# Two heads in one attention step on halves of the matrix array, and adaLN products on four column strips

## The chip, the cores and the metric

The kernel runs on one core of a Trainium2 chip. The metric is device time in microseconds (us) of one execution. Of the kernel before, three runs are shown: 3553.65 us in the median, from 3548.11 to 3559.67. The engines are named as in the profile: PE is TensorE (PEld its weight loads), DVE is VectorE, ACT is ScalarE, POOL is GpSimd, and SP is SyncE, which here only issues transfers.

## What is computed

One inference step of a two-layer encoder trunk, for a prompt of 1024 frames and a sample of 32 frames, which share all weights (width D = 1024). All arithmetic is in fp32. Both groups stand side by side as T = 1056 columns. In short, from the reference:

```python
mod = silu(c) @ w_ada[i] + b_ada[i]                  # six vectors of 1024 per layer, 12 in all, for two rows c
sh1, sc1, gt1, sh2, sc2, gt2 = split(mod, 6)
h = rmsnorm(x, g[0]) * (1 + sc1) + sh1
y = mixer_ab(h) if i % 2 == 0 else mixer_c(h)        # A: 8 heads on 2 kv heads, sinks; B: mLSTM, 4 heads; C: 16 heads
x = x + gt1 * rmsnorm(y, g[1])
h = rmsnorm(x, g[2]) * (1 + sc2) + sh2
x = x + gt2 * rmsnorm(swiglu(h), g[3])

s = q @ k.T * d ** -0.5 + bias                       # attention, head_dim d = 64
m = max(s.max(-1), sink)                             # sink only in A
p = exp(s - m); p = p / (p.sum(-1) + exp(sink - m))  # softmax without sinks in C
o = p @ v
```

In A a block of 128 queries sees up to 256 keys, in C up to 640.

## The kernel before

**Layout and stages.** x, h and all activations lie transposed, features on the 128 partitions and frames along the columns. Projections split both operands into a high and a low part (fp32r) and run three matmuls per block of 128x352 (`project`, lines 670 to 683). The stages follow one another: the inputs are turned and the first norm and the first two adaLN vectors are made (lines 693 to 798); attention A in four pairs of heads (lines 900 to 908); the gates and the four heads of B; the output projection, residual and FFN of layer 0; attention C in eight pairs of heads (lines 1046 to 1082), each with the q, k and v projections of the next pair fed in between; the output projection and FFN of layer 1. Each engine runs a program of its own, written out by hand in the blocks `tensor`, `scalar`, `vector`, `gpsimd` and `sync`, and semaphores with computed counts tie them together.

**Attention.** A pair is two heads, whose q and k lie on partitions 0 to 63 and 64 to 127 of one tile. `attention` (lines 808, 1171 and 1632 on the three engines) takes 18 half steps: nine blocks of rows (eight of 128 prompt frames, one of 32 sample frames) for head 0, then the same for head 1. A half step is: scores on 64 rows of the array (line 824), DVE's reduction that adds the bias, writes the probabilities' exponents and takes the minimum (line 1666), in A another minimum with the sink (1670), ACT's exponential with its sum (1184) and in A a sink term (1183), PE's transposes of the probabilities, one for each block of 128 keys (838), ACT's copy of these to SBUF (1193 to 1196), the product with V, where the transposed probabilities are the stationary operand and 64 columns of V move (850), and DVE's reciprocal and scaling into `o_tok` (1649, 1651). Transposes lag the scores by two half steps in A and by one in C, the product with V by one more. At the end of a pair nine blocks of `o_tok` are turned in two rounds (863), and ACT and DVE write them as high part `o_hi` (1214) and low part `o_lo` (1679).

**What is fed in between.** `fill` is called once per half step on each engine. In A it runs half an adaLN product (`ada_fill`, `ada_products`, lines 763 and 877): the four or eight matmuls of silu(c) (two columns, the stationary operand) with 256 columns of w_ada (line 770). Four such products of eight matmuls make one of the 12 vectors. Their rows are copied by DVE (1522), turned in eight small transposes (781) and added to the bias (1527). Each product's weights are one tile of 1 MB that SP loads into a ring of four when the product four back is done (lines 408 to 414). In C, `fill` runs a third of a 352-column block of the next pair's projection (`qkv_step`, line 1035), and ACT evacuates each finished block (1428) and splits each new weight tile (1110), DVE its low part (1496). The first five fills stand in `pre` (1050 to 1067), between the transposes of the cached keys, of V and of K. The last C pair has no fill.

**Queues.** SP issues w_ada and all weight tiles in program order (lines 416 to 468). POOL loads the bias of each head: in A when the pair's scores are read (562), in C head 0's after nine half steps and head 1's after 18 (615).

Of the kernel before, what the change touches and what calls it, by code (L numbers as in the profile page):

```python
# [11 lines left out]
D = 1024  # L12
# [62 lines left out]
def build(nc, ins, outs):  # L75
# [3 lines left out]
    with ctx:  # L79
# [19 lines left out]
        XE = YF + 2 * HB_  # L99
# [18 lines left out]
        silu_c = small("silu_c", [128, KD, 2])  # L118
# [3 lines left out]
        mins = small("mins", [128, 6])  # L122
        sums = small("sums", [128, 6])
        rsum = small("rsum", [128, 6])
        neg_sink = small("neg_sink", [128, HQ_A])
        sink2 = small("sink2", [128, 2])
        sink_e = small("sink_e", [128, 6])
# [8 lines left out]
        ada_row = at("ada_row", [2, 4, 256], F0)  # L136
# [14 lines left out]
        probs_a = at("probs_a", [128, 3, 256], mx[0])  # L151
        probs = scratch("probs", [128, 2, 640])
        probs_t = scratch("probs_t", [128, 2, 5, 128])
        o_tok = scratch("o_tok", [128, NBLK + 1, 128])
# [47 lines left out]
        ADB = KD * 256 * 4  # L202
        ada_s = [at(f"ada_s{u}", [128, KD, 256], YF + ADB * u) for u in range(4)]
        ada_m = [at(f"ada_m{u}", [128, KD, 256], (YF, R1 + HB_ // 2)[u // 2] + ADB * (u % 2)) for u in range(4)]
# [60 lines left out]
        ada_loaded = [sem(f"ada_loaded{i}") for i in range(4)]  # L265
# [15 lines left out]
        t_done, t_read, o_done, o_read = sem("t_done"), sem("t_read"), sem("o_done"), sem("o_read")  # L281
# [29 lines left out]
        def one(n):  # L311

            return n + 1
# [28 lines left out]
        def key_blocks(kind, p):  # L343
# [8 lines left out]
            "A": dict(n0=0, r0=4, o0=0, pre=0, lag=2, score_bufs=3, fill0=0, probs=probs_a),  # L352
            "C": dict(n0=72, r0=4 + 72, o0=8, pre=4, lag=1, score_bufs=2, fill0=5, probs=probs),
# [9 lines left out]
        def score_bank(kind, n):  # L363
            return 1 + n % 3 if kind == "A" else 1 + 2 * (n % 2)
# [3 lines left out]
        def _(sp):  # L368
# [20 lines left out]
            ada = I["w_ada"].rearrange("l (k p) n -> l p k n", p=128)  # L389
# [18 lines left out]
            def ada_load(ring, layer, q, n):  # L408

                for u in range(4):
                    sp.wait_ge(ada_done, q * 4 + (n + u + 1))
                    c = bass.ds(q * 1024 + ((n + u) * 256 - layer * 6 * D), 256)
                    sp.dma_start(ring[u][:, :, :], ada[layer][:, :, c]).then_inc(ada_loaded[u], 16)

            ada_load(ada_s, 0, 0, 0)
            for i, c in enumerate((COL_KA, COL_VA)):
                load(i, i, plain(w_ab, i, slice(c, c + 128), KD))
            ada_load(ada_s, 0, 1, 0)
# [31 lines left out]
            ada_load(ada_m, 0, 0, 8)  # L451
            q_tile(2)
            ada_load(ada_m, 0, 0, 12)
            q_tile(3)
            with sp.Fori(1, 3) as q:
                ada_load(ada_m, 0, q, 12)
            ada_load(ada_m, 1, 3, 12)
            gates_tile()
            with sp.Fori(4, 6) as q:
                ada_load(ada_m, 1, q, 12)  # L460
            head_tile(0, 0)
            with sp.Fori(6, 9) as q:
                ada_load(ada_m, 1, q, 12)
# [62 lines left out]
        def _(pool):  # L526
# [12 lines left out]

            nc.gpsimd.memset(ones[:, :], 1.0).then_inc(const_done, 1)  # L540
# [26 lines left out]
            pool.wait_ge(ol_done, one(8))  # L567
# [71 lines left out]
            def pair_c(hp, par, last):  # L639
                if not last:  # L640

                    pool.wait_ge(ol_done, one(hp * 2 + 8))
                    apart(pool)
                    caches_c(hp + 1, 1 - par)
# [21 lines left out]
        def _(pe):  # L666
# [26 lines left out]
            pe.sem_inc(ada_done, 4)  # L693
# [67 lines left out]
            pe.wait_ge(const_done, 1)  # L761

            def ada_products(ring, m, half, bank_, copied, loads):

                u = m % 4
                if half == 0:
                    pe.wait_ge(ada_copied, copied)
                    pe.wait_ge(ada_loaded[u], loads)
# [3 lines left out]
                if half == 1:  # L772
                    last.then_inc(ada_done, 1)
# [1240 lines left out]
```

## Time and profile before

| | before |
|---|---|
| median of three runs | 3553.65 us (3548.11 to 3559.67) |
| profiled execution: span from the first to the last instruction | 3540.5 us |
| its own device time | not told apart from the three runs |
| PE busy | 3220.4 us (91%), 18909 matmul passes |
| DVE, ACT, POOL busy | 1218.8, 1037.2, 155.4 us |
| moved by DMA | 201.65 MB, mean 57 GB/s |
| mean granted clock of PE | 0.922 of full speed |

How to read it: a row of a timeline gives start, recorded length, engine, line of the kernel, operation, output<-inputs, shapes and a count. Recorded matmul lengths overlap their successors, so the start of the next group tells what a group cost in the queue. Two PE records stand for one fp32 matmul, three fp32r matmuls for one block of a projection. "128*2 128x256" means a stationary operand of 128 rows and two columns with 256 moving columns. What stands in square brackets is idle time before the instruction and what ended it. The granted clock is 1.00 at 2.4 GHz and 0.50 at 1.2 GHz.

### The profile page before, as it was taken

The numbers are of one execution on the slowest core, as the hardware profiler recorded it, in microseconds if no ns is written. First come the engines' busy times: TensorE is split into PE (matmuls) and PEld (weight loads), VectorE is DVE, ScalarE is ACT, GpSimd is POOL, SyncE is SP. The second block draws the span as 40 slices with busy tenths as digits, with TensorE's granted clock in tenths as the row PEclk, the third lists the DMA queues.
The fourth block names the chain that finished last, engine by engine and source line by source line (L and its number), as shares of the span: only waits on it lengthen the run. The fifth ranks groups of instructions, "written<-read, shape, count | busy, mean of one in ns | idle before, by whom it ended". The sixth has DMA issues, their size and how long they took to land.

```text
span 3540.5 us, 53095 instructions
## 1 busy us (share of the span) xinstructions
PE 3220.4 (91%) x18909; PEld 2904.5 (82%) x18909; DVE 1218.8 (34%) x2578; ACT 1037.2 (29%) x2090; POOL 155.4 (4%) x197
## 2 busy tenths in 40 slices
PE   6999988888679999999949999999994999999997
PEld 4655587787679999999948878788694999999996
DVE  3333333332442232323472222222227232323326
ACT  4322233333241111122243333333224212121123
POOL 2000000000100000000020000000002000000000
PEclk9999988877889999999969999999596999999998
DMA  9444212211101111111121111111020111111111
GB/s 307 134 138 135 89 34 26 26 19 69 36 24 38 51 42 51 45 39 57 36 75 47 41 38 38 38 38 38 13 85 12 42 47 43 52 33 56 48 33 64
DMA packets 279679, 201.65 MB, mean 57 GB/s; under 512 B 25932, under 2 KB 270356, under 8 KB 279156
## 3 DMA queue, kind: packets, MB, share of 16 engines
q1 hardware_dynamic: 271748, 166.31, 16.9%
q0 software_dynamic: 7792, 33.43, 2.8%
q8 instruction: 94, 1.54, 0.2%
q14 instruction: 45, 0.37, 0.0%
HBM read 181.49 MB, written 23.44 MB: 58 GB/s over the span
## 4 chain that ended last, share of the span: by engine, by line
PE 87%; DVE 6%; ACT 2%; issue 2%; DVEq 1%; DMA 1%; POOL 0%; SPq 0%; ACTq 0%; POOLq 0%
PE psum L679 22%; PE psum L680 21%; PE psum L681 21%; PE psum L824 6%; PE psum L770 5%; PE psum L850 5%; PE psum L838 3%; DVE x L1600 2%; DVE norm_buf L1557 1%; DVE diag L1548 1%; DVEq L1610 1%; ACT w_hi L1110 1%; PE psum L738 1%; PE psum L950 1%; PE psum L951 1%
## 5 line engine op out<-in xcount | busy, mean ns | idle before, releaser
L679 PE MATMUL psum<-h_hi,w_hi 128*128 128x352 f32 x3240 | 1081.4, 334 | 47.2 <-DVE w_lo L1496 19.1
L681 PE MATMUL psum<-h_hi,w_lo 128*128 128x352 f32 x3240 | 1053.0, 325 | 2.6 <-issue 2.6
L680 PE MATMUL psum<-h_lo,w_hi 128*128 128x352 f32 x3240 | 1053.4, 325 | 1.9 <-issue 1.9
L679 PEld LDWEIGHTS psum<-h_hi,w_hi 128*128 128x128 f32 x3240 | 620.0, 191 | 79.3 <-issue 31.0
L680 PEld LDWEIGHTS psum<-h_lo,w_hi 128*128 128x128 f32 x3240 | 621.6, 192 | 7.6 <-issue 7.6
L681 PEld LDWEIGHTS psum<-h_hi,w_lo 128*128 128x128 f32 x3240 | 619.3, 191 | 2.8 <-issue 2.8
L1496 DVE TENSOR_TENSOR w_lo<-w_raw,w_hi 128x1024 fp32r<-128x1024 f32 x231 | 282.2, 1224 | 698.1 <-ACT w_hi L1110 698.1
L679 PE MATMUL psum<-ff_hi,w_hi 128*128 128x352 f32 x1056 | 342.5, 324 | 3.9 <-DVE w_lo L1496 3.6
L1110 ACT ACTIVATE w_hi<-w_raw 128x1024 fp32r<-128x1024 f32 x231 | 242.5, 1053 | 353.6 <-PE psum L681 342.3
L680 PE MATMUL psum<-ff_lo,w_hi 128*128 128x352 f32 x1056 | 341.9, 324 | 0.0
L681 PE MATMUL psum<-ff_hi,w_lo 128*128 128x352 f32 x1056 | 341.9, 324 | 0.0
L679 PEld LDWEIGHTS psum<-ff_hi,w_hi 128*128 128x128 f32 x1056 | 199.6, 189 | 5.0 <-issue 5.0
L681 PEld LDWEIGHTS psum<-ff_hi,w_lo 128*128 128x128 f32 x1056 | 199.7, 189 | 0.0
L680 PEld LDWEIGHTS psum<-ff_lo,w_hi 128*128 128x128 f32 x1056 | 199.5, 189 | 0.0
L850 PE MATMUL psum<-v_tok,probs_t 128*128 128x64 f32 (+2 forms) x1264 | 179.7, 281 | 7.5 <-issue 5.7
L1184 ACT ACTIVATE probs<-probs,mins 128x128 f32<-128x128 f32 (+2 forms) x144 | 101.1, 702 | 285.2 <-DVE mins L1666 285.2
L1370 ACT ACTIVATE ff_hi<-ffs 128x352 f32 x126 | 62.8, 498 | 410.7 <-DVE ffs L1897 410.7
L850 PEld LDWEIGHTS psum<-v_tok,probs_t 128*128 128x128 f32 (+2 forms) x1264 | 166.1, 200 | 15.0 <-issue 11.3
L738 PE MATMUL psum<-diag,ones 128*128 128x128 f32 x144 | 37.4, 428 | 150.9 <-DVE diag L1548 150.9
L1897 DVE TENSOR_TENSOR ffs<-sil,psum 128x352 f32<-128x352 f32 x126 | 65.7, 521 | 310.5 <-PE psum L681 310.5
L1366 ACT ACTIVATE sil<-psum 128x352 f32<-128x352 f32 x126 | 58.6, 465 | 369.5 <-PE psum L681 369.5
L1666 DVE CUSTOM_DVE_ANT_0 probs<-psum,neg_bias 128x128 f32<-128x128 f32 (+2 forms) x144 | 95.6, 664 | 191.1 <-PE psum L824 175.0
(307 smaller groups left out, 3547.3 us busy)
## 6 DMA issues: line engine op xcount, KB each, us to landing
ada_m<-in_w_ada SPq DMA_DIRECT2D x40, 1024.0 KB, 5.2
w_raw<-in_w_ffn_gate SPq DMA_DIRECT2D x88, 192.0 KB
w_raw<-in_w_ffn_up SPq DMA_DIRECT2D x88, 192.0 KB
w_raw<-in_w_ffn_down SPq DMA_DIRECT2D x112, 128.0 KB
w_raw<-in_w_in_c SPq DMA_DIRECT2D x48, 192.0 KB
x<-x_spill POOLq DMA_DIRECT2D x2, 4224.0 KB, 12.8
ada_s<-in_w_ada SPq DMA_DIRECT2D x8, 1024.0 KB, 11.3
w_raw<-in_w_ffn_down SPq DMA_DIRECT2D x128, 64.0 KB
```

The source lines that it names most:

```text
L679: nc.tensor.matmul(out, w_hi[:, slot, k], hi[:, k, c], start=(k == 0), stop=False)
L680: nc.tensor.matmul(out, w_hi[:, slot, k], lo[:, k, c], start=False, stop=False)
L681: last = nc.tensor.matmul(out, w_lo[:, slot, k], hi[:, k, c], start=False, stop=(k == kt - 1))
L738: last = nc.tensor.matmul(psum[:, b0 + tt, c:c + 128], ones[:, :], diag[:, turn(n, tt) % 2, i], start=True, stop=True)
L770: last = nc.tensor.matmul(psum[0:2, bank_, 0:256], silu_c[:, k], ring[u][:, k, :], start=(k == 0), stop=(k == KD - 1))
L824: last = nc.tensor.matmul(psum[0:m, score_bank(kind, n) + col // 512, col % 512:col % 512 + kn], lhs, keys(blk, kn, rows, k, kct), start=T ...
L838: last = tr(tps[0:kn, s, 0:m], c["probs"][0:m, n % sb, 128 * s:128 * s + kn], ident[0:m, 0:m])
L850: last = nc.tensor.matmul(oacc[0:m, 0:64], probs_t[0:kn, n % 2, s, 0:m], v, start=(s == 0), stop=(s == len(kb) - 1))
L1110: A(w_hi[:, slot], w_raw[:, slot], ACT.Copy).then_inc(hi_done, 1)
L1184: A(probs[0:m, n % sb, 0:w], probs[0:m, n % sb, 0:w], ACT.Exp, scale=-1.0, bias=mins[0:m, n % 6:n % 6 + 1], accum_out=sums[0:m, n % 6:n % ...
L1496: V.tensor_tensor(w_lo[:, slot], w_raw[:, slot], w_hi[:, slot].bitcast(F32), ALU.subtract).then_inc(lo_done, 1)
L1666: op = V.tensor_tensor_reduce(out=probs[0:m, n % sb, 0:w], in0=sc, in1=neg_bias[0:m, e, c0:c0 + w], scale=1.0, scalar=3.0e38, op0=ALU.add, ...
```

## The change

**Attention.** A step now handles both heads of one block of rows, so a pair has nine steps and a tenth without scores. Scores of the two heads alternate, piece by piece, on rows 0 to 63 and 64 to 127, into PSUM banks 1-2 and 3-4. DVE reduces both, then waits for both exponentials and scales the probabilities themselves by the reciprocal of their sum (in A with the sink's term), before they are turned. The product with V has V (64 columns) as the stationary operand and the transposed probabilities as 128 moving columns; the two heads alternate on columns 0 to 63 and 64 to 127, and the output comes out already turned. `o_tok` and its final transposes are gone; ACT and DVE write `o_hi` and `o_lo` for one block of rows in every step. In A, the sink's term is the exponential of a difference (`sink_gap`) that DVE makes with one more small operation per step. Fills stand at two fixed spots per step (three in the first and last step of C). Transposes and product with V lag by one step in A and C alike.

**adaLN.** A slab of w_ada is now 128 rows by 1024 columns (0.5 MB, rows of 4 KB), in a ring of eight. A group is four matmuls of 256 columns, one per column strip of 32; silu(c) is padded with zeros to 32 columns. Eight groups make a vector, whose result lies on four strips and is turned in two transposes of 128x128. At the start all eight groups of the first vector run ahead of the first sum of squares, and all of the second after the third.

**Waits.** In C, POOL loads both heads' biases after the eighth step. Each pair's `pre` waits for the last copy of the pair before, not for its `o_lo`.

The core of the diff (the sizes of small buffers, semaphore counts of later stages and unchanged loops are cut):

```diff
-        ada_s = [at(f"ada_s{u}", [128, KD, 256], YF + ADB * u) for u in range(4)]
+        ada_s = [at(f"ada_s{k}", [128, D], YF + 4096 * k) for k in range(KD)]
...
+        FILLS = {"A": [(1, 2)] * 10, "C": [(0, 1, 2)] + [(1, 2)] * 8 + [(0, 1, 2)]}
...
+            def ada_load(ring, q):
+                for k in range(KD):
+                    if q:
+                        sp.wait_ge(ada_done, KD * (q - 1) + k + 1)
+                    sp.dma_start(ring[k][:, :], I["w_ada"][q // 6, 128 * k:128 * k + 128, D * (q % 6):D * (q % 6) + D]
+                                 ).then_inc(ada_loaded[k], 16)
...
-                    pool.wait_ge(scores_read, hp * 18 + (CREDIT + 72 - 18 + 9 * (e + 1)))
+                    pool.wait_ge(scores_read, hp * 18 + (CREDIT + 72 - 18 + 17 + e))
...
+            def ada_products(ring, q, k, bank_):
+                if k == 0:
+                    pe.wait_ge(ada_copied, one(q))
+                pe.wait_ge(ada_loaded[k], q * 16 + 16)
+                for u in range(4):
+                    last = nc.tensor.matmul(psum[32 * u:32 * u + 32, bank_, 0:256], silu_c[:, k], ring[k][:, 256 * u:256 * u + 256],
+                                            start=(k == 0), stop=(k == KD - 1))
+                last.then_inc(ada_done, 1)
...
+            for k in range(KD):
+                ada_products(ada_s, 0, k, 3)
+            sum_x(0, 0, 0)
+            ada_transposes(0, 5)
+            spread(0, 0, 0)
+            sum_x(0, 1, 0)
+            spread(0, 1, 0)
+            sum_x(0, 2, 0)
+            for k in range(KD):
+                ada_products(ada_s, 1, k, 4)
+            ada_transposes(1, 5)
+            spread(0, 2, 0)
...
@@ attention, tensor block @@
+                for i in range(10):
+                    if i < 9:
+                        m = qrows(i)
+                        pe.wait_ge(scores_read, N(i) * 2 + CREDIT)
+                        cuts = cut_scores(kind, i)
+                        col = 0
+                        for s, (blk, kn) in enumerate(cuts):
+                            for e in range(2):
+                                rows = slice(64 * e, 64 * e + 64)
+                                last = nc.tensor.matmul(psum[0:m, score_bank(e) + col // 512, col % 512:col % 512 + kn],
+                                                        q[rows, 128 * i:128 * i + m], keys(blk, kn, rows, k, kct), start=True, stop=True)
+                                if s == len(cuts) - 1:
+                                    last.then_inc(scores, 1)
+                            col += kn
+                    work(i, 0)
+                    if i:
+                        turned(i - 1, 0)
+                    work(i, 1)
+                    if i:
+                        turned(i - 1, 1)
+                    work(i, 2)
+                    if i:
+                        n, m = i - 1, qrows(i - 1)
+                        pe.wait_ge(t_read, R(2 * n + 2))
+                        pe.wait_ge(ol_done, one(N(n)))
+                        kb = key_blocks(kind, n)
+                        for s, (blk, kn) in enumerate(kb):
+                            for e in range(2):
+                                cols = slice(64 * e, 64 * e + 64)
+                                v = vc[0:kn, blk[1], cols] if isinstance(blk, tuple) else vt[0:kn, blk, cols]
+                                last = nc.tensor.matmul(oacc[cols, 0:m], v, probs_t[0:kn, e, s, 0:m],
+                                                        start=(s == 0), stop=(s == len(kb) - 1))
+                        last.then_inc(o_done, 1)
...
@@ attention, scalar block @@
+                for i in range(10):
+                    work(i, 0)
+                    if i:
+                        copy(i - 1, 0)
+                    if i < 9:
+                        exps(i, 0)
+                    work(i, 1)
+                    if i < 9:
+                        exps(i, 1)
+                    if i:
+                        copy(i - 1, 1)
+                    work(i, 2)
+                    if i:
+                        act.wait_ge(o_done, N(n) + 1)
+                        A(tile_of(o_hi, it)[:, :, 128 * n:128 * n + m], oacc[:, 0:m].unsqueeze(1), ACT.Copy).then_inc(oh_done, 1)
...
@@ attention, vector block, after the two reductions of step i @@
+                    if i < 9:
+                        dve.wait_ge(exp_done, N(i) * 2 + 2)
+                        V.reciprocal(rsum[0:m, b, :], total[0:m, b, :])
+                        for e in range(2):
+                            V.tensor_scalar(probs[0:m, b, e, 0:w], probs[0:m, b, e, 0:w], rsum[0:m, b, e:e + 1], None,
+                                            ALU.mult).then_inc(p_done, 1)
+                    work(i, 1)
+                    work(i, 2)
+                    if i:
+                        dve.wait_ge(oh_done, N(n) + 1)
+                        V.tensor_tensor(tile_of(o_lo, it)[:, :, cs], oacc[:, 0:m].unsqueeze(1), tile_of(o_hi, it)[:, :, cs].bitcast(F32),
+                                        ALU.subtract).then_inc(ol_done, 1)
```

## Rows read from the trace of the kernel before

**Rows 1.** The page: its span, and the chain that ended last by engine.
```profile
span 3540.5 us, 53095 instructions
...
PE 87%; DVE 6%; ACT 2%; issue 2%; DVEq 1%; DMA 1%; POOL 0%; SPq 0%; ACTq 0%; POOLq 0%
```

**Rows 2.** Windows: length; busy PE, PEld, DVE, ACT, POOL; granted clock; DMA share; GB/s.
```profile
27.00:104.00 77.00, 61.88 (x325) 41.86 (x323) 27.22 (x34) 37.03 (x50) 18.92 (x12) 0.89 0.88 280
206.00:273.00 67.00, 63.45 (x335) 31.38 (x333) 27.59 (x123) 19.79 (x77) 1.07 (x2) 0.98 0.52 163
629.00:639.00 10.00, 8.19 (x59) 6.45 (x58) 4.58 (x24) 5.47 (x24) 0.00 (x0) 1.00 0.00 1
1954.00:2039.00 85.00, 82.34 (x508) 67.86 (x507) 24.88 (x77) 33.67 (x76) 5.81 (x12) 1.00 0.14 40
2480.00:2572.00 92.00, 84.64 (x293) 59.39 (x293) 22.51 (x75) 25.80 (x64) 2.60 (x4) 0.51 0.04 12
```

**Rows 3.** The timeline of one half step of attention A, PE, ACT and DVE.
```profile
222.31 0.44 PE L838 MATMUL psum<-ident,probs_a 128*128 128x128 f32 x2
...
222.58 0.56 PE L850 MATMUL psum<-v_tok,probs_t 128*128 128x64 f32 x4
222.78 0.38 ACT L1193 ACTIVATE probs_t<-psum 128x256 f32<-128x256 f32 x1 [2.15 <-PE psum L838]
223.06 0.28 ACT L1183 ACTIVATE sink_e<-sink,mins 128x1 f32<-128x1 f32 x1
...
223.07 0.70 PE L824 MATMUL psum<-k_a,q_a 64*128 64x256 f32 x2
...
223.25 0.49 ACT L1184 ACTIVATE probs_a<-probs_a,mins 128x256 f32<-128x256 f32 x1
...
223.64 0.19 ACT L1184 ACTIVATION_READ_ACCUMULATOR probs_a<-probs_a,mins 128x1 f32 x1
...
223.69 1.89 PE L770 MATMUL psum<-ada_m,silu_c 128*2 128x256 f32 x8
223.95 0.42 DVE L1666 CUSTOM_DVE_ANT_0 probs_a<-psum,neg_bias 128x256 f32<-128x256 f32 x1
...
224.46 0.16 DVE L1670 TENSOR_TENSOR mins<-mins,sink 128x1 f32<-128x1 f32 x1
...
225.51 0.44 PE L838 MATMUL psum<-ident,probs_a 128*128 128x128 f32 x2
```

**Rows 4.** The PE timeline: the first scores and the last output transposes of one A pair.
```profile
205.73 0.46 PE L824 MATMUL psum<-k_a,q_a 64*128 64x128 f32 x2 [0.87 <-ACT q_a L1168]
...
271.31 1.14 PE L863 MATMUL psum<-ident,o_tok 128*128 128x128 f32 x4 [1.88 <-DVE o_lo L1679]
```

**Rows 5.** The PE timeline of a C step: scores of 512 columns, then projection matmuls.
```profile
2007.97 1.12 PE L824 MATMUL psum<-k_c,q_c 64*128 64x512 f32 x2
2009.02 0.43 PE L679 MATMUL psum<-h_hi,w_hi 128*128 128x352 f32 x1
2009.29 0.32 PE L680 MATMUL psum<-h_lo,w_hi 128*128 128x352 f32 x1
2009.44 0.32 PE L681 MATMUL psum<-h_hi,w_lo 128*128 128x352 f32 x1
```

**Rows 6.** Groups by line and shape: count, busy us, mean ns of one, idle before.
```profile
L1110 ACT ACTIVATE w_hi<-w_raw 128x1024 fp32r<-128x1024 f32 x231 | 242.5, 1053 | 353.6 <-PE psum L681 342.3 <-DMA w_raw<-in_w_in_ab 11.3
...
L1184 ACT ACTIVATE probs<-probs,mins 128x640 f32<-128x640 f32 x64 | 53.0, 829 | 144.6 <-DVE mins L1666 144.6
L1193 ACT ACTIVATE probs_t<-psum 128x640 f32<-128x640 f32 x64 | 44.5, 696 | 12.8 <-PE psum L838 12.8
...
L1774 DVE TENSOR_SCALAR conv_t<-u_k,conv_h 128x1059 f32<-128x1059 f32 x4 | 3.1, 773 | 24.4 <-issue 15.9 <-ACT q_b L1292 8.5
```

**Rows 7.** The PE timeline of the start: third sum of squares, products of the second vector.
```profile
47.38 0.83 PE L719 MATMUL psum<-ones,norm_buf 128*128 128x1 f32 x6
...
55.17 10.52 PE L770 MATMUL psum<-ada_s,silu_c 128*2 128x256 f32 x48
```

More of the change, by code:

```diff
@@ L361, in num_bank, with score_bank, fills, tile_of @@
             return 0 if c % 2 else 7
-        def score_bank(kind, n):
-            return 1 + n % 3 if kind == "A" else 1 + 2 * (n % 2)
+        def score_bank(e):
+            return 1 + 2 * e
+        FILLS = {"A": [(1, 2)] * 10, "C": [(0, 1, 2)] + [(1, 2)] * 8 + [(0, 1, 2)]}
+        def fills(kind, i, spot):
+            if spot not in FILLS[kind][i]:
+                return None
+            return (5 if kind == "C" else 0) + sum(len(f) for f in FILLS[kind][:i]) + FILLS[kind][i].index(spot)
+        def tile_of(t, i):
+            return t[:, bass.ds(i, 1) if not isinstance(i, int) else slice(i, i + 1), :]
         @block.sync
@@ L809, in attention, with work @@
                 c = KINDS[kind]
[L810 removed]
+                N = lambda n: it * 9 + (c["n0"] + n)
                 R = lambda n: it * (18 + c["pre"]) + (c["r0"] + c["pre"] + n)
[L812 to L819 removed]
+                def work(i, spot):
+                    f = fills(kind, i, spot)
+                    if fill and f is not None:
+                        fill(f)
@@ new lines, in turned @@
+                def turned(n, e):
+                    m, first = qrows(n), c["slots"][e]
+                    pe.wait_ge(p_done, N(n) * 2 + (e + 1))
+                    pe.wait_ge(t_read, R(2 * n + (e if kind == "C" else 0)))
+                    apart(pe)
+                    for s, (_, kn) in enumerate(key_blocks(kind, n)):
+                        last = tr(tps[0:kn, first + s, 0:m], c["probs"][0:m, (n + par) % 2, e, 128 * s:128 * s + kn], ident[0:m, 0:m])
+                    last.then_inc(t_done, 1)
@@ new lines, in copy, with work @@
+                        A(probs_t[0:TS, e, full, 0:m], tps[0:TS, first + full, 0:m], ACT.Copy).then_inc(t_read, 1)
+                def work(i, spot):
+                    f = fills(kind, i, spot)
+                    if fill and f is not None:
+                        fill(f)
+                pre()
+                for i in range(10):
[11 more added lines that the diff above has]
+                    if i:
+                        n, m = i - 1, qrows(i - 1)
+                        act.wait_ge(o_done, N(n) + 1)
+                        A(tile_of(o_hi, it)[:, :, 128 * n:128 * n + m], oacc[:, 0:m].unsqueeze(1), ACT.Copy).then_inc(oh_done, 1)
@@ new lines, in attention, with work @@
+                N = lambda n: it * 9 + (c["n0"] + n)
+                probs = c["probs"]
+                def work(i, spot):
+                    f = fills(kind, i, spot)
+                    if fill and f is not None:
+                        fill(f)
+                for i in range(10):
+                    if i < 9:
+                        m, (w, c0) = qrows(i), score_width(kind, i)
+                        b = (i + par) % 2
+                        mn = mins[0:m, b, :]
+                        for e in range(2):
+                            if i == 0:
+                                if kind == "A":
+                                    dve.wait_ge(bias_raw[e], it * 16 + 16)
+                                else:
+                                    dve.wait_ge(bias_ok[e], it + 1)
+                            dve.wait_ge(scores, N(i) * 2 + (e + 1))
+                            b_ = score_bank(e)
+                            sc = psum[0:m, b_:b_ + 2, :].rearrange("p b c -> p (b c)")[:, 0:w]
+                            apart(dve)
+                            op = V.tensor_tensor_reduce(out=probs[0:m, b, e, 0:w], in0=sc, in1=neg_bias[0:m, e, c0:c0 + w],
+                                                        scale=1.0, scalar=3.0e38, op0=ALU.add, op1=ALU.min, accum_out=mn[:, e:e + 1])
+                            if not sinks:
+                                op.then_inc(scores_read, 1)
```

344 lines of the change are left out of this document (108 added, 236 removed).

## The prediction

> **What bounds the kernel now.** I read the page first: a span of 3540.5 us, with TensorE on 87% of the chain that ended last [rows 1]. So a gain must come out of TensorE's own queue, in the stages that the diff touches. The windows over those stages came next [rows 2]: the start; one pair of attention A (67 us, TensorE busy 63.45); one pair of attention C (85 us, busy 82.34); and the last C pair, which has no projection beside it (92 us, at a granted clock of 0.51, the 1.2 GHz level). All other stages keep their instructions and so their time. Last came the timeline of single steps: from the start of one group on TensorE to the start of the next is what the group costs in the queue.
>
> **The prices.** A product in plain fp32 is two weight loads and two passes. In A a score of 256 columns holds the queue from 223.07 to 223.69, 0.62 us; eight adaLN passes of 256 columns 1.82, so 0.2275 each; two transposes 0.27; four passes with V 0.49 [rows 3]. In C a score of 512 columns takes 1.05 [rows 5]. Both scores fit two passes at 0.83 ns a column and 0.2 us to begin, which makes 1.27 for 640 columns. No row shows two matmuls on different strips of the array in flight together, so the price that decides is bounded from both sides: nothing overlaps, or the strips run wholly side by side. Two strips with one product each then last 3 passes for 4, four strips 5 for 8, and n products alternating with n on the other strip 2n+1 for 4n.
>
> The Trainium skill (TensorE: Matmul & The Clock Gate, part 3) states that matmuls on other row or column groups start some 4 ns apart, and that three column strips measured 2.38 times one. By that an adaLN group of 1.82 us would last about 1.82 x 3 / (4 x 2.38) = 0.57 us (an estimate from that page), which is the side of the first rival below.
>
> **Attention A.** One step now holds both heads. TensorE: scores 3 passes of 0.21 and 0.2 to begin, 0.83; two adaLN groups of 5 x 0.2275, 2.28; four transposes 0.54; V with two key blocks 5 passes for 8, each of 128 moving columns and so about half an adaLN pass, 0.115: 0.58. Together 4.2 us. The chain of waits is now longer than that: from the scores' end 0.18 to VectorE; its two reductions 0.42 and 0.51 (to the start of the minimum); the minimum 0.16; the added sink gap 0.24 with its drain; ScalarE's sink term 0.19 and two exponentials of 0.58; the copy of the second head's transposes, which stands behind them on ScalarE, 0.28; 0.15 to TensorE (estimate); V 0.58; the next scores 0.83. That is 4.7 [rows 3]; I take 4.85 with the semaphores between. VectorE's scaling moves from the output to the probabilities: twice 256 columns at 0.73 ns by the nearest scaling [rows 6], 0.4 us, over before the next scores end; without that cover it would cost 0.4 a step. A short first step (3.4), eight of 4.85 and a tail of 3.2, in which the output's transposes are gone, make 45.4. Before, the first score starts at 205.73 and the last output transpose ends at 272.1 [rows 4]: 66.4, and the other three pairs repeat it. Gain 21 a pair, **84 us** in four. If nothing overlaps, TensorE sets the step: 1.04 + 3.64 + 0.54 + 0.92 and the beginnings, 6.3; 59 a pair, 7.5 below before, mostly the tail. If all overlaps, only the chain is left: 42.
>
> The weight slabs: 10 MB a pair in 45 us are 233 GB/s. The start moved 280 at a DMA share of 0.88, A now moves 163 at 0.52 [rows 2]. Bytes and ring stay; each slab is half a tile, in rows of 4 KB, with twice the issues on SP's queue, and has eight groups, some 20 us, to land. I cost this at nothing, covered by those groups; if 200 GB/s were all, it would cost 7 us a pair.
>
> **Attention C, seven pairs with projections.** Scores before, by the prices above, nine steps of two heads: 18.1 us. After: 3 passes up to 512 columns, 3 x 0.427 + 2 x 0.107 = 1.49 for 640, each with 0.2 to begin: 12.3. Gain 5.8. V: 120 passes at 0.1225 become 68 at 0.115, and the sample's 20 short ones 11: gain 7.4. The ten output transposes fall away: 1.0. Against that stands a wait: V needs the second copy, and ScalarE's queue before it is copy, exponential, exponential, copy, 0.70 + 0.92 + 0.92 + 0.70. This is about as long as the transposes and two fills beside it on TensorE, but in half of the steps a projection's evacuation (352 columns, about 0.45 by the 640-column copy), and twice a pair a weight split (1.05), falls in between [rows 6]: 3.5 a pair, between 0 and 5.3. VectorE's dearer scaling (0.9 a step) and the two small output copies gate only work that is a step away. On POOL's queue both bias loads of the next pair now wait for the eighth step; the ninth step and the next pair's five fills (40 matmuls of 0.16, 6.5 us [rows 5]) cover 0.66 MB, 4 us at A's 163 GB/s. Net 10.7 a pair, **75 us**. With no overlap: one score start less a step (1.8), no output transposes, and the wait in return, about 1 a pair. With full overlap 15.
>
> **The last C pair** runs at the low clock, where every pass takes twice the time. Its step is the whole chain: at 640 columns transposes 1.1, copy 0.7, two exponentials 1.84, copy 0.7, V 2.5, scores 3.2 and 0.4 of semaphores, 10.4; the narrow steps start at 5.4. The window of 92 us becomes about 87: **5 us**. Without overlap 108; at the high clock and wholly side by side 58.
>
> **The start.** The second modulation vector stands in the queue as 48 passes in 10.5 us from 55.17, after 16 before them. Now 33 passes follow the third sum of squares, which ends at 48 [rows 7], at the low clock at first, and end near 57.4 in place of 65.7: **8 us**. Without overlap 1, and nothing if its slabs land late.
>
> Sum: 84 + 75 + 5 + 8 = 172, a span of 3368.5. The profiled execution's own time isn't told apart from the three runs; their median lies 13 us above its span. With that, **3381 us**. About 0.3% (11 us) is what a measurement of this kernel can tell from no change.
>
> **Rivals.**
> *Whole overlap*: a strip's second pass doesn't hold back the other strip. A gains 24 a pair (97), C 15 (106), the last pair 13, the start 10: 226, so **3328**. The order in the queue speaks against it.
> *A falls to the low clock*: with a chain longer than TensorE's work, the engine idles in each step. For staying high: from 629 to 639 the clock was at 1.00 with 8.19 of 10 us busy. Against: the last pair stayed at 0.51 with 84.64 of 92 busy [rows 2]. TensorE's 4.2 us become 8.4 a step, 78 a pair, 12 above before: 8 - 48 + 75 + 5 = 40, so **3514**.
> *It doesn't do what it says*: the strips take turns. A 30, C 7, the last pair -16, the start 1: 22, so **3531**, give or take 15.
> *Slower: each change of strip costs a refill.* After a score on half the array the next matmul has 0.27 to its successor, the one after it 0.15 [rows 5]: a price of 0.11. Before, that comes once per head and step. Now the strips alternate: in a C pair 28 times in the scores and 70 in V, in an A pair 20, 34 and 80 in adaLN, in the start 64; 8 x 98 + 4 x 134 + 64 = 1384. At 0.11 these are 152 us on top of the turns: **3683**. It ends slower from 0.016 us a change on. Only that row speaks for it, and there the shape of the weights changes too, not the strip alone.
> The Trainium skill (TensorEngine Tiling (Array Packing), key properties) says that changing the tiling mode drains the engine, and not just changing the tile; by that rule the alternations cost nothing.
>
> **How the numbers follow.** Pairwise overlap 0.52, whole overlap 0.12, A at the low clock 0.12, turns 0.13, refill 0.11. The range, 3322 to 3525, takes the first three (0.76) with their bounds, transfers at 200 GB/s (28 us) among them, and the quick edge of the turns. Faster: the first three and two thirds of the turns, 0.85; within 0.3% the rest of the turns, 0.04; slower 0.11.
>
> **What would show it.** Right: in a C step the second head's first pass starts before the first head's second ends, and both heads at 640 columns take near 1.7 us; an adaLN group near 1.1; A pairs of 45 us, with TensorE's longest wait on the probabilities' copy; C pairs of 75. Wrong: groups still at 1.8 and 2.5 us (turns) or above (refill), or a granted clock near 0.5 in A. A DMA share near 0.9 in A with TensorE waiting for slabs would say that the transfers bind.

## The result, and the profile after

The changed kernel takes 3296.98 us (median; 3285.35 to 3299.18) against 3556.48 us before on the same chip (3548.11 to 3559.67), a ratio of 0.927 (95% interval 0.924 to 0.930). The direction was forecast, the size was not: 3297 lies under the low end of the range, 3322. The profiled execution took 3285.35 us, 1.65 us more than its span.

The page of the changed kernel, its span and its chain by engine:

```profile
span 3283.7 us, 52354 instructions
...
PE 81%; DVE 7%; ACT 5%; issue 3%; DVEq 1%; DMA 1%; another core or an unknown queue 0%; POOL 0%; ACTq 0%; SPq 0%
```

Against [rows 1] the span is 256.8 us shorter, and TensorE's share of the chain fell from 87 to 81%: the chain now runs over VectorE and ScalarE more often. The windows that answer to [rows 2], with the same columns (start, an A pair, part of a C pair, the last C pair):

```profile
27.00:68.00 41.00, 18.16 (x168) 12.52 (x166) 21.42 (x28) 20.94 (x23) 17.93 (x10) 0.67 0.93 339
...
168.00:224.00 56.00, 42.21 (x380) 25.57 (x380) 23.35 (x110) 21.85 (x80) 1.08 (x2) 0.97 0.62 203
1768.00:1828.00 60.00, 57.95 (x450) 47.41 (x450) 25.24 (x74) 30.17 (x76) 4.30 (x10) 1.00 0.14 39
...
2253.70:2314.70 61.00, 42.27 (x267) 26.40 (x267) 23.10 (x73) 23.72 (x65) 2.60 (x4) 0.70 0.04 10
```

A kept the high clock (0.97), with TensorE idle for a quarter of the time; C is still full of TensorE (57.95 of 60); the last pair's clock is 0.70 where it was 0.51. Slabs come at 203 GB/s and a DMA share of 0.62: the transfers don't bind.

Where the time went, by the start of the first instruction of each stage on TensorE (us; the rows add up to the spans):

| stretch | before | after | difference | forecast |
|---|---|---|---|---|
| to the first projection | 77.9 | 68.4 | -9.5 | -8 |
| A, first score of pair 1 to that of pair 4 | 248.3 | 165.7 | -82.6 | -63 |
| A, first score of pair 4 to B's state transposes | 139.5 | 112.9 | -26.6 | -21 |
| B, from there to the first output product | 331.8 | 338.7 | +6.9 | 0 |
| C, seven pairs, first score to the last pair's | 605.7 | 485.6 | -120.1 | -75 |
| the last C pair, first score to the output product | 85.7 | 61.0 | -24.7 | -5 |
| all the rest | 2051.6 | 2051.3 | -0.2 | 0 |

The timeline of one A step (PE, ACT, DVE; it answers to [rows 3]):

```profile
195.50 0.70 PE L843 MATMUL psum<-k_a,q_a 64*128 64x256 f32 x4
...
196.13 0.44 PE L829 MATMUL psum<-ident,probs_a 128*128 128x128 f32 x2
...
196.41 0.42 DVE L1662 CUSTOM_DVE_ANT_0 probs_a<-psum,neg_bias 128x256 f32<-128x256 f32 x1
...
196.72 0.64 PE L775 MATMUL psum<-ada_m,silu_c 128*32 128x256 f32 x8
...
197.29 0.44 PE L829 MATMUL psum<-ident,probs_a 128*128 128x128 f32 x2
...
197.72 0.20 ACT L1187 ACTIVATE sink_e<-sink_gap 128x2 f32<-128x2 f32 x1 [0.72 <-DVE sink_gap L1670]
197.83 0.49 ACT L1188 ACTIVATE probs_a<-probs_a,mins 128x256 f32<-128x256 f32 x1
...
198.81 0.36 ACT L1196 ACTIVATE probs_t<-psum 128x256 f32<-128x256 f32 x1
...
199.31 0.66 PE L865 MATMUL psum<-probs_t,v_tok 128*64 128x128 f32 x8 [1.02 <-ACT probs_t L1196]
199.41 0.62 DVE L1682 TENSOR_SCALAR probs_a<-probs_a,rsum 128x256 f32<-128x256 f32 x2
...
199.90 0.70 PE L843 MATMUL psum<-k_a,q_a 64*128 64x256 f32 x4
```

Read the starts. Both heads' scores take 0.63 us (195.50 to 196.13), as one head's did; eight adaLN passes 0.57 (196.72 to 197.29) where they took 1.82; V of both heads 0.59. This step is 4.40 us, as most of a pair are (the first three of this pair are 3.66, 5.25 and 4.80), and TensorE idles 1.02 of it because the second head's transposes, done at 197.7, are copied behind the sink term and both exponentials, at 198.81.

The PE timeline of a C step (V of four blocks, scores of 640 columns, transposes) shows the same:

```profile
1862.28 1.09 PE L865 MATMUL psum<-probs_t,v_tok 128*64 128x128 f32 x16 [0.16 <-ACT probs_t L1196]
1863.30 1.35 PE L843 MATMUL psum<-k_c,q_c 64*128 64x512 f32 x8
1864.58 0.76 PE L829 MATMUL psum<-ident,probs 128*128 128x128 f32 x5
```

Two heads' scores of 640 columns take 1.28 us; the forecast priced one head at 1.27 and both at 1.7. In the single records, which don't name a strip but tell the heads apart by their starts, the second head's first pass begins 6 ns after the first head's (1863.308 after 1863.302), and both second passes follow at 1863.835 and 1863.842.

The start: the second vector's 64 passes need 5.9 us, beginning partly at the low clock (48 took 10.52 in [rows 7]):

```profile
50.27 5.86 PE L775 MATMUL psum<-ada_s,silu_c 128*32 128x256 f32 x64
```

### The profile page after: what moved, and what is told of

It reads as the page before. It is cut to its first block, busy times and chain, and to the rows that moved or that the text cites. A ratio compares the mean times of both kernels' runs of the same rounds, so it can differ in the third digit from the quotient of the medians.

```text
span 3283.7 us, 52354 instructions
## 1 busy us (share of the span) xinstructions
PE 2900.5 (88%) x18729; PEld 2690.7 (82%) x18729; DVE 1208.8 (37%) x2494; ACT 1027.5 (31%) x2138; POOL 155.8 (5%) x198
## 4 chain that ended last, share of the span: by engine, by line
PE 81%; DVE 7%; ACT 5%; issue 3%; DVEq 1%; DMA 1%; another core or an unknown queue 0%; POOL 0%; ACTq 0%; SPq 0%
PE psum L686 23%; PE psum L688 22%; PE psum L687 22%; PE psum L865 3%; PE psum L843 3%; PE psum L829 2%; DVE x L1605 2%; ACT probs L1188 1%; DVE norm_buf L1566 1%; ACT probs_a L1188 1%; DVE diag L1557 1%; ACT w_hi L1115 1%; ACT probs_t L1196 1%; PE psum L744 1%; DVE w_lo L1501 1%
## 5 line engine op out<-in xcount | busy, mean ns | idle before, releaser
L744 PEld LDWEIGHTS psum<-diag,ones 128*128 128x128 f32 x144 | 31.9, 320 | 161.0 <-DVE diag L1557 161.0
L1927 DVE TENSOR_TENSOR y_ffn<-y_ffn,psum 128x352 f32 (+1 forms) x192 | 99.4, 520 | 169.6 <-PE psum L688 166.5
L865 PE MATMUL psum<-probs_t,v_tok 128*64 128x128 f32 (+2 forms) x1264 | 97.3, 289 | 48.7 <-ACT probs_t L1196 48.3
L865 PEld LDWEIGHTS psum<-probs_t,v_tok 128*64 128x64 f32 (+1 forms) x1264 | 72.8, 143 | 82.2 <-issue 81.7
## 6 DMA issues: line engine op xcount, KB each, us to landing
x<-x_spill POOLq DMA_DIRECT2D x2, 4224.0 KB, 13.8
```

What stands on the lines that cost most here:

```text
L744: last = nc.tensor.matmul(psum[:, b0 + tt, c:c + 128], ones[:, :], diag[:, turn(n, tt) % 2, i], start=True, stop=True)
L865: last = nc.tensor.matmul(oacc[cols, 0:m], v, probs_t[0:kn, e, s, 0:m], start=(s == 0), stop=(s == len(kb) - 1))
L1927: V.tensor_tensor(dst, dst, src, ALU.add).then_inc(evac_dve, 1)
```

## The experiments

The theory after this reading: strips of the array run wholly side by side, and that is the gain. The rivals: it comes from the shorter pipeline (nine steps for eighteen, no output transposes), or, for adaLN, from the slabs. The diffs of this section are shortened.

**Attention alone** (the kernel after, with the old adaLN whole: its loads, products, copies and order at the start; in A its products go to bank 4, its transposes to bank 0):

```diff
-    matmul(psum[32*u:32*u+32, bank_, 0:256], silu_c[:, k], ring[k][:, 256*u:256*u+256])   # four strips, slabs
+    matmul(psum[0:2, bank_, 0:256], silu_c[:, k], ring[u][:, k, :])                       # one strip, tiles
```

> The attention steps with both heads as in the changed kernel, the adaLN products as before (one strip, two columns of weights, tiles of 1 MB, eight passes in 1.82 us). Theory (strips run wholly side by side; in A the chain of waits sets the step of 4.40 us and TensorE idles about 1.2 us in it): two groups of eight passes cost 2 x 1.25 us more a step, of which 1.2 fill the idle time, so A gains back about 1.3 us x 9 steps x 4 pairs = 47 us, and the start its 9.5: about 3355 us. Rival (the shorter pipeline alone gives the gain in A, adaLN is hidden there anyway): only the start comes back, 3307. Rival (all of the gain in A is adaLN's): A comes back whole, 3297 + 109 + 9.5 = 3415.

3336.27 us; ratio to before 0.943 (0.938 to 0.947), about 3353 on the scale of the result. The first and third A pair are 67.3 and 67.2 us from first score to first score (54.9 in the kernel after), so 12.4 x 4 = 50 came back, as the theory said (47); the start 12. The second pair takes 76.0 (55.9 after). Ahead of its projection TensorE pauses, and the trace names no cause:

```profile
255.96 0.65 PE L690 MATMUL psum<-h_hi,w_hi 128*128 128x352 f32 x1 [6.08 <-issue]
```

Counted with this spot, A as a whole is 58 us longer than in the kernel after. The total meets the 3355 expected by luck: stage B, which no kernel here touches (below), is 17 us shorter in this profile.

**adaLN alone** (the kernel before with the new adaLN code, the same lines the other way round).

> The kernel before with only the adaLN products on four column strips by weight slabs. Theory: TensorE sets A's half steps there, so the 1.25 us saved in each of 20 groups a pair come out nearly whole: 4 x 20 to 25 us, and 9.5 at the start: about 3460 us, A pairs near 59 us from first score to first score. Rival (the slabs' format or their transfers give the gain, the strips don't): A no quicker than the 233 GB/s of slabs allow, about 3545 with groups still at 1.8 us. C and the last pair stay as before in both.

3427.45 us; ratio 0.968 (0.964 to 0.971), about 3441 on the scale of the result, 19 less than expected. A pairs 57.6, 61.0 and 56.3 us, the top of what the theory expected; C stays at 85.4. So in A adaLN alone takes 23.8 of the first pair's 81.4 us, attention alone 14.1, and both together 26.5: each removes work that the other would have hidden. From the first score of a pair to the end of the last this kernel needs 31.7 us, the kernel after 36.8: the merged step is the slower pipeline in A, and makes up for it in its tail. Both end the first pair's attention at the same time (42.6 and 42.5 us after its first score); what the kernel after gains beyond that is the projection behind the pair, 12.5 us for 15.0 (see the part on attention A below).

**All on one strip** (attention's second head and all adaLN products moved onto the first strip, all else as after):

```diff
-    rows = slice(64 * e, 64 * e + 64)                       # scores
+    rows = slice(0, 64)
-    matmul(oacc[64*e:64*e+64, 0:m], v, probs_t[..])         # V
+    matmul(psum[0:64, 7, 128*e:128*e+m], v, probs_t[..])
-    matmul(psum[32*u:32*u+32, bank_, 0:256], ..)            # adaLN
+    matmul(psum[0:32, bank_, 256*(u%2):256*(u%2)+256], ..)
```

> The changed kernel with the same instructions in the same order, but all of them on one strip: both heads' scores on the array's rows 0 to 63 (head 1 uses head 0's queries and keys), both heads' products with V into columns 0 to 63, and all four adaLN products of a group into strip 0, added up in pairs. The output differs in those parts. Theory (the gain is the overlap of strips): adaLN groups at 1.82 us, both scores of 640 columns at 2.5, V of five blocks at 2.4; A's step is TensorE's and near 6.3 us (+17 us a pair, 68), C +15 a pair (105), the start +9, the last pair +20 to +40: about 3500 to 3530 us. Rival (it is the shorter pipeline: nine steps for eighteen, no output transposes, division ahead of V): at most 3330.

3500.07 us; ratio 0.986 (0.981 to 0.992). The PE timeline of a C step, as above:

```profile
1974.89 1.93 PE L865 MATMUL psum<-probs_t,v_tok 128*64 128x128 f32 x16 [0.16 <-ACT probs_t L1197]
1976.76 2.43 PE L843 MATMUL psum<-k_c,q_c 64*128 64x512 f32 x8
1979.11 0.77 PE L829 MATMUL psum<-ident,probs 128*128 128x128 f32 x5
```

The same instructions take 1.87 and 2.35 us where they took 1.02 and 1.28. The first and third A pair are 73.2 and 73.1 us (+18.3), the second, with a pause of 6.9 us as in the run with attention alone, 81.8; most C pairs are 82.9 (+14.3), the first projection starts 15.5 later, the last pair takes 76.2 (+15.2). So about 210 of the 257 us are the overlap of strips (the ratio rises from 0.927 to 0.986, the profiled span by 214); the shorter pipeline by itself is worth some 8 us in an A pair without the pause (2.3 of it the clock of the projection behind it, below), 2.5 in a C pair, and 9.5 in the last.

**Slabs on one strip** (of the three edits above only that of adaLN; modulations differ).

> The changed kernel with its slabs of weights, their loads and their waits as they are, but all four adaLN products of a group into strip 0 (added up in pairs, so the modulations differ); attention as in the changed kernel. It parts the strips from the slabs. Theory (the strips alone give the adaLN part its gain): groups at 1.82 us, A pairs near the 67.3 us of the run with attention alone changed, first projection at 80 us or later. Rival (the slabs' format or their rows of 4 KB give it): A pairs near 55 and the first projection near 68.

3369.92 us (one run; before beside it 3545.34). The PE timeline in A:

```profile
202.50 1.91 PE L775 MATMUL psum<-ada_m,silu_c 128*32 128x256 f32 x8
204.35 0.33 PE L829 MATMUL psum<-ident,probs_a 128*128 128x128 f32 x1
```

A group is back at 1.85 us, the first and third A pair at 66.9 (the second, with the same pause, at 75.5) and the first projection at 84.4. The slabs' format gives adaLN nothing; the strips give it all.

**By head** (the loops exchanged; in scores and V):

```diff
-    for s, blk in enumerate(blocks):
-        for e in range(2):
+    for e in range(2):
+        for s, blk in enumerate(blocks):
```

> The changed kernel with the loops over heads and pieces exchanged: in a step all pieces of head 0's scores come before head 1's, and all blocks of head 0's products with V before head 1's. Nothing else differs, and in A the scores are one piece, so their order stays. Theory a (products are handed out in order, a product waits until its own strip is free and holds back all behind it): head 1's scores of 640 columns start only when head 0's second piece starts, 1.28 us become about 2.1, and V's five blocks 1.02 become about 1.85; C pairs gain back some 1.6 us in the wide steps, about 11 us a pair, the last pair 10 to 15, A under 3: about 3390 us. Theory b (each strip has a queue of its own): no change, 3297. Theory c (the order is passes, one by one): head 1 starts with head 0's last pass, 640 columns take 2.4 us, and 3410 results.

3315.36 us; ratio 0.937 (0.934 to 0.940), some 34 us above the kernel after by the ratios; most C pairs 73.0 (+4.4). None of the three theories holds as it stood. (The 1.02 us that the expectation gives to V's five blocks are those of four; five take 1.25 in the kernel after.) The PE timeline of two steps (V of four blocks and scores of 640; V of five):

```profile
1790.77 1.55 PE L865 MATMUL psum<-probs_t,v_tok 128*64 128x128 f32 x16 [0.16 <-ACT probs_t L1196]
1792.26 1.36 PE L843 MATMUL psum<-k_c,q_c 64*128 64x512 f32 x8
1793.54 0.77 PE L829 MATMUL psum<-ident,probs 128*128 128x128 f32 x5
...
1797.67 2.02 PE L865 MATMUL psum<-probs_t,v_tok 128*64 128x128 f32 x20
1799.62 0.71 PE L843 MATMUL psum<-k_c,q_c 64*128 64x512 f32 x2
```

Scores still take 1.28 us, though all four passes of head 0 stand ahead of head 1's; V of four blocks takes 1.49 (1.02 before the exchange), of five 1.95 (1.25). The single records tell why; two passes that start within 20 ns of each other must be on different strips, as in the run with all on one strip such passes start 0.11 us apart or more. In the scores head 1 starts 13 ns after head 0, with three passes of head 0 still waiting. In V of three, four and five blocks (6, 8 and 10 passes a head) head 1 starts 6 ns after head 0's third, fifth and seventh pass: each time when three of head 0's passes are left to start, and so in all such groups of full blocks in this trace. A pass is handed out ahead of waiting ones of another strip, as long as no more than three wait.

**adaLN strip by strip** (two slabs at a time; four passes a strip in a row):

```diff
-    for u in range(4):
-        matmul(strip u, slab k)
+    if k % 2:
+        for u in range(4):
+            for kk in (k - 1, k):
+                matmul(strip u, slab kk)
```

> The changed kernel with the adaLN products taken two slabs at a time and strip by strip: each strip gets its four passes (two products) in a row, then the next strip. In A the groups come in every second fill, twice as long. It tells what lets a pass start ahead of others that wait: by the run with the loops exchanged, another strip's first pass starts once no more than three passes wait. If that is counted over the whole array: strip 1 starts with strip 0, strips 2 and 3 only as the queue drains, near 0.5 and 0.7 us later, and sixteen passes last 1.4 to 1.9 us. If each strip holds three waiting passes of its own: all four strips start within 0.05 us, and sixteen passes last about 1.1. The time stays within 15 us of the changed kernel in either case.

3307.56 us (one run). The windows of one such group, adaLN's line alone (length, PE busy and count of passes under way, PEld likewise, clock, DMA):

```profile
172.51:172.56 0.05, 0.05 (x4) 0.05 (x6) 1.00 0.00 0
172.56:172.75 0.19, 0.19 (x4) 0.13 (x8) 1.00 0.00 0
172.75:172.80 0.05, 0.05 (x8) 0.04 (x4) 1.00 0.00 0
```

Four passes start at 172.514, .528, .541 and .554, and the next four only from 172.754: all four strips began within 0.04 us, and the last of sixteen starts 0.71 after the first; where products with V follow at once, such a group costs 1.02 us, of about 1.1 expected. So each strip keeps its own three waiting passes. The spacing, 13 ns for four passes a strip and 6 to 7 for two, puts the handing out at about 3.3 ns a pass.

**What binds A now: three steps and the kernel after again**, five rounds on one chip.

```diff
 # first: ScalarE's queue in a step (C: the copy between the exponentials)
     copy(i - 1, 0)
+    copy(i - 1, 1)
     exps(i, 0)
     exps(i, 1)
-    copy(i - 1, 1)
 # second, also: in A TensorE turns both heads ahead of both adaLN groups
 # third, also: VectorE subtracts the output of step i - 2, ahead of its wait for the exponentials
-    o_lo(i - 1)      # at the end of step i
+    o_lo(i - 2)      # after the sink gap of step i
```

> The changed kernel with the second copy of transposes further ahead on ScalarE: in A ahead of the sink term and both exponentials, in C between the two exponentials. Theory (in the changed kernel a wait, the copy behind the exponentials, sets A's step and part of C's and the last pair's): TensorE's 48 us of waits for the probabilities' copy nearly go, but in A the copy waits for transposes that stand behind a group of adaLN products and so delays the exponentials by 0.4 us; VectorE's round of reductions, exponentials, scaling and output then sets a step of about 4.3 in place of 4.40: 4 us over four pairs. C up to 2 us a pair, the last pair 6 us: about 12 us less than the changed kernel. Rival (TensorE's queue sets the step): no change in A and C.

> As the run before, and in A both heads' transposes ahead of both groups of adaLN products on TensorE, so that the copy doesn't hold up the exponentials. Theory: A's step is VectorE's round without that 0.4: 3.9 us, 0.5 x 9 x 4 = 18 us less in A than the changed kernel, and C as in the run before. Rival (the slabs of weights bind A): TensorE waits for them there and the step stays at 4.3.

> As the run before, and VectorE subtracts a step's output one step later, in the time in which it waits for the exponentials. Theory: its round is 0.3 shorter, A's step 3.6: 29 us less in A than the changed kernel, and some 40 in all, near 3257 on the scale of its 3297. Rival (slabs): as in the run before.

> The changed kernel once more, on the chip of the three others, to compare them: 0.927 of the time of before.

| | us, median | ratio to before | A, pair 1 to 4 | C, seven pairs | last pair |
|---|---|---|---|---|---|
| after again | 3301.55 | 0.9285 (0.9265 to 0.9305) | 165.8 | 485.9 | 57.7 |
| first | 3277.12 | 0.922 (0.920 to 0.924) | 161.6 | 477.0 | 53.2 |
| second | 3269.53 | 0.919 (0.917 to 0.922) | 156.7 | 477.2 | 53.1 |
| third | 3256.63 | 0.915 (0.913 to 0.917) | 150.1 | 477.3 | 53.2 |

The groups of V's products by line in the kernel after, then in the first of the three (busy us, mean ns, idle before and its releaser):

```profile
L865 PE MATMUL psum<-probs_t,v_tok 128*64 128x128 f32 (+2 forms) x1264 | 97.3, 289 | 48.7 <-ACT probs_t L1196 48.3
```

```profile
L865 PE MATMUL psum<-probs_t,v_tok 128*64 128x128 f32 (+2 forms) x1264 | 94.6, 284 | 6.0 <-ACT probs_t L1196 6.0
```

The wait of 48.3 us is down to 6.0, and yet A's three pairs gain 4.2 only: TensorE's longest wait in A is now for VectorE's scaled probabilities (24.6 us, 4.1 in the kernel after again), so VectorE's round sets the pace, as expected. Most steps fall to 3.85 us (4.3 expected), but from its last score to its end the first pair takes 7.4 us where it took 5.9. C gains 8.9 in seven pairs and the last pair 4.5 (14 and 6 were the most expected). The total gains 24 us by the medians, 16 by the spans of the profiles; 12 were expected. The second and third edit aim at VectorE's round and gain 4.9 and 6.6 more in A's three pairs, of 11 and 8 expected. A part of that is clock: one projection behind a pair takes 14.1 us in the first kernel and one 15.0 in the second, where the others take 12.5. By the attention alone, first score to last product with V, the three edits gain 5.8, 6.1 and 3.9 us in three pairs. The third kernel's windows row and its PE timeline in A:

```profile
166.00:216.00 50.00, 40.10 (x377) 26.35 (x378) 22.77 (x110) 21.75 (x79) 1.11 (x2) 0.97 0.68 227
```

```profile
192.57 0.66 PE L868 MATMUL psum<-probs_t,v_tok 128*64 128x128 f32 x8
...
193.16 0.70 PE L843 MATMUL psum<-k_a,q_a 64*128 64x256 f32 x4
...
196.91 0.41 PE L843 MATMUL psum<-cache_akt,q_a 64*32 64x128 f32 x4
```

This step is 3.75 us (193.16 to 196.91), the others from a pair's third on 3.3 to 4.1 (3.6 expected), with slabs at 227 GB/s and no wait for them. By the medians this kernel takes 45 us less than the kernel after beside it, where 40 were expected; the spans of the two profiles differ by 33, as the profiled execution of the kernel after was its quickest (3290.01).

**Stage B** has the same instructions in all kernels, and took 331.8 us before, 338.7 after, 321.3 with attention alone, 346.1 in the kernel after run again, and 352.7 with adaLN by strip. The windows of its shortest and its longest (attention alone; adaLN by strip):

```profile
464.00:785.00 321.00, 272.83 (x1452) 244.47 (x1448) 117.75 (x319) 113.71 (x307) 19.89 (x31) 0.79 0.22 22
```

```profile
399.00:752.00 353.00, 294.93 (x1453) 265.79 (x1451) 118.14 (x320) 115.61 (x307) 19.99 (x31) 0.73 0.20 20
```

The instructions are the same; the granted clock is 0.79 and 0.73. Two profiles of the same kernel after differ by 7.4 us there. So the 6.9 us that this stage lost are no effect of the change that these runs can show.

## Why the prediction was wrong, step by step

**The step that failed** is the price between the bounds: "the second pass of one strip holds back the first pass of the next strip until it begins itself". A waiting pass holds back the other strip only when three of its own strip wait already; with products that alternate, each strip's waiting passes fill up evenly and both strips keep running. The forecast price of 3 passes for 4 and 5 for 8 is in truth near 2 for 4 and 2 for 8: an adaLN group 0.57 us instead of 1.14, both scores of 640 columns 1.28 instead of 1.7. The rival "whole overlap" (226 us, 3328) was the right mechanism, at a chance of 0.12; "the order in the queue speaks against it" was the wrong argument, since no row showed two strips in flight.

By its speed-up of three column strips the Trainium skill (TensorE: Matmul & The Clock Gate, part 3) gave an estimate of 0.57 us for an adaLN group; this case's trace has 0.57. Its figure of 4 ns between starts on different strips stands beside 6 to 7 ns here for products of two passes. The same part says that matmuls start strictly in program order; by head, a pass of the second head started ahead of three earlier ones of the first, so here the measurement decides against it.

**Attention A** (21 a pair forecast, 24 by whole overlap, 26.5 to 29.2 measured). The chain was right in its sum: with everything overlapped "only the chain is left: 42", and from the first score at 168.57 to the end of the last V at 210.68 it is 42.1. The rest was not in the sum at all. The windows of a pair's tail and of the projection that follows it, in the kernel before and then in the kernel after:

```profile
186.00:190.90 4.90, 2.21 (x13) 1.39 (x13) 1.40 (x4) 0.70 (x1) 0.00 (x0) 0.79 0.58 197
190.90:195.50 4.60, 4.60 (x16) 4.54 (x17) 0.67 (x2) 0.52 (x1) 0.00 (x0) 0.50 0.02 4
195.50:205.70 10.20, 9.37 (x58) 9.07 (x57) 0.00 (x0) 1.73 (x4) 0.00 (x0) 0.99 0.00 0
```

```profile
151.00:156.10 5.10, 4.20 (x56) 1.98 (x55) 2.06 (x13) 2.23 (x12) 1.08 (x2) 1.00 0.70 220
156.10:160.70 4.60, 4.60 (x33) 4.60 (x30) 0.31 (x2) 0.66 (x2) 0.00 (x0) 1.00 0.88 305
160.70:168.50 7.80, 7.12 (x45) 6.83 (x43) 0.00 (x0) 1.11 (x3) 0.00 (x0) 1.00 0.06 24
```

Before, in the tail of output transposes TensorE was busy 2.21 of 4.90 us; the next projection's first 4.6 us ran at 0.50, the 1.2 GHz level, and have 16 records. Now TensorE is busy 4.20 of 5.10 us in the tail, and the projection runs at 1.00 from its first matmul and has 33. That is 2.3 us a pair (14.75 to 12.47 from its start to the next score). The run with adaLN alone, which keeps the old tail, bears it out: the first 4.6 us of its first three projections have 0.50, 0.50 and 0.70, and the three take 13.8 to 15.3 us. With the new tail 24 of 30 take 12.5 us; of the other six, three stand behind the pauses of 6 to 7 us in the runs with adaLN on one strip. So the tail is the likely cause, though no run changed it alone. The pair with 29.2 also had, before, 3.12 us ahead of its projection for which the trace names no cause (0.79 after, a wait for `mod`). It is the spot of the pauses of 6 to 7 us, the turn of the loop that holds two pairs; what makes them was not settled. The case *A falls to the low clock* looked at the same resource from the wrong side: the new idle of 1.02 us a step didn't lower the clock (0.97 in A), while behind the old tail it was low.

**Attention C** (10.7 a pair forecast, 15 by whole overlap, 16.7 to 18.6 measured). Besides the overlap, the added wait was charged too high: 3.5 a pair. TensorE idles 2.05 us of 60 after and 2.66 of 85 before; 0.8 of the 60 is put down to the copy, and taking the copy ahead of the second exponential gains 1.1 a pair.

**The last pair** (5 forecast, 24.7 measured). "Runs at the low clock" failed: the clock rose to 0.70. On one strip the pair gains 9.5 at a clock that rose as well (0.75), where the forecast had it 16 slower; the overlap is the other 15.2. Both are rough: with the same instructions the new pair took 57.7 to 62.2 us in five profiles. That TensorE, busy 80.81 of 84.50 us, stayed at 0.50 before, and is granted more while busy 42.27 of 61, was seen in all runs with the new step; what lets the clock rise there was not settled.

**The start** (8 forecast, 9.5 measured) came out near by luck: the products of the second vector took 5.9 us where the forecast had 9.4 (48 to 57.4), for the same wrong price, but they began at 50.3 and not at 48, as the third sum of squares ended later. The transfers (nothing forecast, nothing measured) were right, as was TensorE's longest wait in A, on the probabilities' copy. In C, POOL loads the biases at the ninth step's two reductions, a step later than the texts ahead of the result say; the trace puts no wait of VectorE in C down to them. *Turns* and *refill* are out: 1.28 us for both scores leaves no room for either.

By terms: A 109 for 84, C 120 for 75, the last pair 25 for 5, the start 10 for 8, B and the rest -7 for 0: 257 for 172. Of the 85 us missed, 54 are whole for pairwise overlap (226 - 172); the clock of the projections after A, the wait in C and the clock of the last pair are the other gains, less B's 7.

## What to carry to other kernels

Products with 64 rows, or with 64 or fewer output partitions, are worth pairing on different strips of the array: two or four fp32 products then cost what one costs, as long as no more than four passes (two products) of a strip stand ahead of the next strip's first: alternate per product, or per two. Once TensorE's part shrinks, look at which queue the next operand stands in: here one copy behind two exponentials cost 48 us of waits, but taking 42 of them away gained 16 to 24 us; the next 8 and 13 (medians) came with edits aimed at VectorE's round, which had become the limit in A. Ask of a pipeline's tail also at what clock the stage behind it starts.

## What the runs showed of the hardware

- Passes of fp32 products on different strips start 6 to 7 ns apart, and 13 ns with four passes a strip handed out: 3.3 ns a pass.
- Each strip keeps three passes waiting beside the running one, and only the next one blocks what stands behind it: seen with two strips (4, 6, 8 and 10 passes); with four strips of four passes nothing was held back.
- On one strip the same instructions cost the full sum: 2.35 us for 1.28, 1.87 for 1.02, 1.85 for 0.57.
- Stage B, unchanged, took 321 to 353 us at granted clocks of 0.79 to 0.73: differences of up to 0.9% of this kernel can come from there alone.
